# A router with its weights held still in two column halves, a re-ordered head loop, and row sums taken from the writing operations

## What is computed

```python
def layernorm(x, g, b):                    # mean and variance over the 1024 columns
    return (_normalize(x) * g + b).astype(x.dtype)

def modulate(x, shift, scale):
    return (_normalize(x) * (1.0 + scale) + shift).astype(x.dtype)
...
    merged = jnp.concatenate([rmsnorm(lru_out, norm_lru_g), rmsnorm(attn_out, norm_attn_g)], axis=-1)
    return merged @ w_out
...
    # router, for each of 256 tokens: 4 groups and 32 experts, 36 logits
    g_prob = jax.nn.softmax((xc @ w_rg + b_rg), axis=-1)
    g_top, g_idx = lax.top_k(g_prob, 1)
    e_logits = (xc @ w_re + b_re).reshape(-1, N_GROUPS, EXPERTS_PER_GROUP)
    e_in = jnp.take_along_axis(e_logits, g_idx[:, :, None], axis=1)[:, 0]
    e_top, e_loc = lax.top_k(jax.nn.softmax(e_in, axis=-1), EXPERT_TOPK)
    # two experts a token, each a gated hidden layer of 256, weighted and summed
...
        x = layernorm(DEEPNORM_ALPHA * x + g1 * mix, ln1_g[l], ln1_b[l])
        u2 = modulate(x, sh2, sc2)
        ffn = hierarchical_moe(u2, ...)
        x = layernorm(DEEPNORM_ALPHA * x + g2 * ffn, ln2_g[l], ln2_b[l])
```

## Time and profile before

| | us |
|---|---|
| median of 3 runs (lowest, highest) | 1044.45 (1040.17, 1044.59) |
| the profiled execution | 1041.96 |
| its span in the trace | 1039.5 |
| TensorE busy | 998.6 |
| VectorE busy | 586.4 |
| ScalarE busy | 351.8 |

### The profile page before, as it was taken

The page is one execution under the profiler, slowest core; times in us unless marked ns, Lnnn a source line. Parts: engine busy times, 40 slices in busy tenths (PEclk is TensorE's granted clock), DMA queues, the critical chain, the costliest instruction groups (busy, mean ns, idle before and its releaser), DMA issues.

```text
span 1039.5 us, 15072 instructions
## 1 busy us (share of the span) xinstructions
PE 998.6 (96%) x5378; PEld 608.9 (59%) x5378; DVE 586.4 (56%) x1104; ACT 351.8 (34%) x676; POOL 20.3 (2%) x41
## 2 busy tenths in 40 slices
PE   8999999999999999999999999989999999999985
PEld 7678556978878534434434579867763343433434
DVE  5834436555345546454454575886765755555556
ACT  5654325346334222222222365743521111111113
POOL 1000001000000000000000000000000000000000
PEclk9999999999998999999999999998899999999998
DMA  9263591456408399999999729530709999999931
GB/s 364 113 258 126 211 416 63 162 191 235 162 24 368 152 378 426 427 424 426 424 427 424 314 82 364 203 122 1 283 10 367 427 425 424 426 424 427 425 157 42
DMA packets 28896, 289.06 MB, mean 278 GB/s; under 512 B 3080, under 2 KB 5544, under 8 KB 7728
## 3 DMA queue, kind: packets, MB, share of 16 engines
q1 hardware_dynamic: 25344, 282.04, 65.9%
q0 software_dynamic: 1136, 3.74, 1.1%
q10 hardware_dynamic: 2368, 2.64, 0.8%
HBM read 287.34 MB, written 1.06 MB: 277 GB/s over the span
## 4 chain that ended last, share of the span: by engine, by line
PE 55%; DVE 7%; ACT 2%; issue 1%; DVEq 0%; ACTq 0%
PE bank L981 22%; PE bank L995 11%; PE bank L1001 6%; PE bank L988 4%; PE bank L626 2%; PE bank L628 1%; PE bank L627 1%; DVE ring_r L483 1%; PE bank L603 1%; PE bank L1103 1%; PE bank L954 1%; PE bank L1104 1%; PE bank L1056 1%; PE bank L925 1%; PE bank L1092 0%
## 5 line engine op out<-in xcount | busy, mean ns | idle before, releaser
L981 PE MATMUL bank<-ring,arena 128*64 128x512 f32 x1040 | 237.5, 598 | 1.4 <-DVE arena L2224 1.4
L2238 DVE TENSOR_REDUCE arena<-bank 128x512 f32 x130 | 83.8, 686 | 117.2 <-PE bank L1001 114.7
L483 DVE TENSOR_TENSOR ring_r<-ring,ring_r 128x1024 fp32r<-128x1024 f32 (+1 forms) x84 | 99.2, 1212 | 84.7 <-ACT ring_r L476 84.7
L981 PEld LDWEIGHTS bank<-ring,arena 128*64 128x64 f32 x1040 | 69.3, 136 | 123.8 <-issue 123.8
L995 PE MATMUL bank<-ring,arena 128*64 128x512 f32 x520 | 125.8, 604 | 0.5 <-DVE arena L2253 0.3
L476 ACT ACTIVATE ring_r<-ring 128x1024 fp32r<-128x1024 f32 (+1 forms) x84 | 85.0, 1046 | 76.9 <-PE bank L628 75.1
L626 PE MATMUL bank<-HT_r,ring_r 128*128 128x256 f32 x352 | 101.6, 289 | 3.5 <-DVE ring_r L483 1.8
L628 PE MATMUL bank<-HT_r,ring_r 128*128 128x256 f32 x352 | 99.6, 283 | 0.0
L1574 ACT ACTIVATE arena<-bank 128x512 f32<-128x512 f32 x64 | 38.3, 598 | 150.8 <-PE bank L981 150.8
L1001 PEld LDWEIGHTS bank<-tab,arena 128*128 128x128 f32 x520 | 55.7, 140 | 54.8 <-issue 49.6
L1001 PE MATMUL bank<-tab,arena 128*128 128x128 f32 x520 | 70.9, 279 | 3.3 <-DVE arena L2267 2.1
(11 more groups left out here) (431 smaller groups left out, 1427.9 us busy)
## 6 DMA issues: line engine op xcount, KB each, us to landing
ring<-in_experts SPq DMA_DIRECT2D x64, 2048.0 KB, 15.1
ring<-in_experts SPq DMA_DIRECT2D x64, 1024.0 KB, 11.5
ring<-in_ada SPq DMA_DIRECT2D x12, 2048.0 KB, 10.4
ring<-in_win SPq DMA_DIRECT2D x5, 2048.0 KB, 13.0
ring<-in_hy SPq DMA_DIRECT2D x3, 2048.0 KB, 19.7
ring<-in_mk SPq DMA_DIRECT2D x2, 2048.0 KB, 13.2
ring<-in_mv SPq DMA_DIRECT2D x2, 2048.0 KB, 10.5
ring<-in_wo SPq DMA_DIRECT2D x2, 2048.0 KB, 7.5
```

Of the source, the lines that this page charges most:

```text
L483: nc.vector.tensor_tensor(R(w), w, R(h), ALU.subtract).then_inc(sem("w_low"), 1)
L981: last = mm(gu_bank[g:g + WIN, :], xw[:, k, :], w[:, k * 512:(k + 1) * 512], start=k < 2, stop=k >= KD - 2)
L2238: last = V.reduce_sum(ysT[:, 4 * u:4 * u + 4, bass.ds(s, WIN)], dT_bank[u][:, :].rearrange("p (c g w) -> p c w g", c=4, g=2), AXX)
```

## The change

Five things are edited. The router product takes eight products of 256 tokens, with 64 columns of weights held still (36 of this k, the rest of the next, whose results are not read), even and odd k in the two column halves. ScalarE copies the result to `turned`, and two products with the table `stack` add the two halves and turn tokens back to the partitions, in a stage of its own (`rl`, bank 3). xn_high, xn_low and the weights w1, w2 move in the orders of ScalarE and VectorE. The number of `occupy` products changes in four places. The orders of ScalarE and VectorE in the head loop are others. The row sums of two norms come from the operations that write X.

```diff
 def moe(b):   # TensorE
-                    occupy("rT2", 0, 19)
+                    occupy("rT2", 0, 17)
...
                 for k in range(KD):
                     ready(pe, f"rT{b}", k // 2)
-                    for t in range(TT):
-                        last = mm(ps[:, t * 64:t * 64 + G + NE], HT[:, k, t * P:(t + 1) * P], w[:, k, :],
-                                  start=k + t == 0, stop=k == KD - 1 and t == TT - 1)
+                    g = 64 * (k % 2)
+                    n = min(64, KD * (G + NE) - k * (G + NE))
+                    last = mm(ps[g:g + n, 0:S], wr[:, b - 1, k * (G + NE):k * (G + NE) + n], HT[:, k, :],
+                              start=k < 2, stop=k >= KD - 2)
                 full(last, f"rt{b}")
+                ps = take(pe, f"rl{b}")
+                ready(pe, f"rt{b}")
+                for t in range(TT):
+                    last = mm(ps[:, t * 64:t * 64 + G + NE], turned[:, t * P:(t + 1) * P], stack[:, 0:G + NE],
+                              start=True, stop=True)
+                full(last, f"rl{b}")
                 if b == 1:
                     ada_col(9)
-                occupy(f"cnt{b}", 0, 10 if b == 2 else 6)
+                occupy(f"cnt{b}", 0, 10 if b == 2 else 8)
@@ TensorE, beside(h)
-                elif h == 3:
-                    occupy("ap2", 0, 4)
                 elif h in (4, 5):
                     if h == 4:
-                        occupy("ap2", 0, 4)
+                        occupy("ap2", 0, 2)
@@ ScalarE, moe(b)
-                for t in range(TT):
-                    A_(R(xn_high[:, t, :]), XN[:, t, :], ACT.Copy).then_inc(sem("xn_high"), 1)
+                A_(R(xn_high[:, 0, :]), XN[:, 0, :], ACT.Copy).then_inc(sem("xn_high"), 1)
+                ps = got(act, f"rt{b}")
+                free(A_(turned, ps[:, 0:S], ACT.Copy), f"rt{b}")
+                A_(R(xn_high[:, 1, :]), XN[:, 1, :], ACT.Copy).then_inc(sem("xn_high"), 1)
@@ ScalarE, head loop
+                if h in (2, 4, 6):
+                    attention_out(h // 2 - 1)
+                if h == 5:
+                    high(act, "wp1", (2,))
                 if h + 2 < H1:
                     a_exp(h + 2)
-                if h in (2, 4, 6):
-                    attention_out(h // 2 - 1)
...
-                if h == 5:
-                    high(act, "wp1", (2,))
@@ ScalarE, statistics(i, t): the next two go, and all four (i, t) are done here
-                link(A_(junk2, X[:, t, :], ACT.Copy, accum_out=sum_z[i, t]))
-                A_(mean_z[i, t], sum_z[i, t], ACT.Copy, scale=-1.0 / D).then_inc(sem("mean"), 1)
@@ VectorE, moe(b): split_low(t) is L2118 and L2119 for one t
+                split_low(0)
+                ps = got(dve, f"rl{b}")
...              (the chain to M12, m2 and cand4)
+                split_low(1)
...
-                (the wait for the exponentials and L2154 to L2159)
                 ps = got(dve, f"cnt{b}")
...              (counts, places, sel)
+                (the wait for the exponentials and L2154 to L2159, now ahead of selw)
@@ VectorE, wp_attention(t)
                     free(V.scalar_tensor_tensor(out=x, in0=ps[:, :], scalar=rstd_a[:, t:t + 1], in1=x,
-                                                op0=ALU.mult, op1=ALU.add), *MIX[t, u])
+                                                op0=ALU.mult, op1=ALU.add, accum_out=(sum_z, half_z)[u][1, t]), *MIX[t, u])
                 for u in range(2):
                     ready(dve, *MIX[t, u])
+                V.tensor_scalar(mean_z[1, t], sum_z[1, t], half_z[1, t], -1.0 / D, ALU.add, ALU.mult).then_inc(sem("mean"), 1)
@@ VectorE, head loop, behind probT2 and a_norm(h + 1)
+                if h == 3:
+                    dve.wait_ge(sem("roots"), upto(ROOTS, "lru"))
+                    wp_lru(0, (0,))
+                    wp_lru(0, (1,))
                 if h + 2 < H1:
                     a_max(h + 2)
                 h = 0: gate_weights(0, 2)                      (as before)
-                h = 1: gate_weights(0, 3), low(wp1, 0 and 1), gate_weights(1, 2), gate_weights(1, 3), lss
+                h = 1: low(wp1, 0), gate_weights(0, 3)
-                h = 2: attention_low(0), low(wp0, 2), wp_lru(0, 0)
+                h = 2: lss, gate_weights(1, 2), attention_low(0)
-                h = 3: wp_lru(0, 1), low(wp0, 3)
-                h = 4: attention_low(1)
+                h = 4: low(wp1, 1), attention_low(1), low(wp0, 2), gate_weights(1, 3)
-                h = 5: low(wp1, 2)
+                h = 5: low(wp0, 3), low(wp1, 2)
                 h = 6: attention_low(2), low(wp1, 3), wp_lru(1, 0)   (as before)
                 h = 7: wp_lru(1, 1), asa                             (as before)
@@ VectorE, mid_norm(t) and behind it
                 V.scalar_tensor_tensor(out=X[:, t, :], in0=XN[:, t, :], scalar=rstd_n[1][:, t:t + 1],
-                                       in1=ROW[:, 1024:2048], op0=ALU.mult, op1=ALU.add).then_inc(sem("x_mid"), 1)
+                                       in1=ROW[:, 1024:2048], op0=ALU.mult, op1=ALU.add, accum_out=sum_z[2, t]
+                                       ).then_inc(sem("x_mid"), 1)
                 dve.wait_ge(sem("x_mid"), t + 1)
+                V.tensor_scalar(mean_z[2, t], sum_z[2, t], -1.0 / D, None, ALU.mult).then_inc(sem("mean"), 1)
-            moments_of(2, 1)
```

More of the change, by code:

```diff
@@ L193, in _moe_stages @@
     one = b == 1
-    return [(f"rT{b}", 4)] + [("adac8", 1)] * one + [(f"rt{b}", 1)] + [("adac9", 1)] * one \
+    return [(f"rT{b}", 4)] + [("adac8", 1)] * one + [(f"rt{b}", 1), (f"rl{b}", 1, (3,))] + [("adac9", 1)] * one \
         + [(f"cnt{b}", 1)] + [("bias", 1)] * one + [(f"gx{b}", 8), (f"swT{b}", 2)] \
@@ L370, in two_blocks @@
         oneh, relb, brow = HTf[:, 0:512], HTf[:, 512:512 + H1], HTf[:, 1024:1536]
+        turned = area(0, S)
         route_at = at + 6656
@@ L918, in moe @@
                 pe.wait_ge(sem("wr"), 16 * b)
-                w = three(wr[:, b - 1, :], KD)
                 ps = take(pe, f"rt{b}")
@@ L1742, in statistics @@
                 A_(dev_n[i][:, t:t + 1], ssq_z[i, t], ACT.Sqrt, scale=1.0 / D, bias=eps_2).then_inc(sem("dev"), 1)
-            for t in range(TT):
-                for u in range(2):
-                    ready(act, *MIX[t, u])
-                statistics(1, t)
-            act.wait_ge(sem("x_mid"), 1)
-            statistics(2, 0)
-            deviation_of(2, 1)
+            for i in (1, 2):
+                for t in range(TT):
+                    statistics(i, t)
             link(A_(idle, eps_2, ACT.Exp))
@@ L2116, in moe, with split_low @@
                 channel_evac(f"rT{b}", HT, 4, gain, shift)
-                for t in range(TT):
+                def split_low(t):
                     dve.wait_ge(sem("xn_high"), TT * (b - 1) + t + 1)
@@ L2124, in moe @@
                 lg = three(ps[:, 0:128], TT)[:, :, 0:G + NE]
-                free(V.tensor_tensor(L, lg, biasr[b - 1].unsqueeze(1).broadcast_to([P, TT, G + NE]), ALU.add), f"rt{b}")
-                ready(dve, f"rt{b}")
+                free(V.tensor_tensor(L, lg, biasr[b - 1].unsqueeze(1).broadcast_to([P, TT, G + NE]), ALU.add), f"rl{b}")
+                ready(dve, f"rl{b}")
                 lgg = L[:, :, 0:G]
@@ L2175, in moe @@
                                            op0=ALU.is_equal, op1=ALU.add).then_inc(sem(f"sel{b}"), 1)
+                dve.wait_ge(sem("e_exp"), b)
+                dve.wait_ge(sem("g_exp"), b)
+                link(V.reduce_sum(gsum, gex, AXX))
+                link(V.reciprocal(pgrp, gsum))
+                link(V.tensor_scalar(w2, ex2, 1.0, None, ALU.add))
+                link(V.reciprocal(w1, w2))
+                link(V.tensor_tensor(w1, w1, pgrp, ALU.mult))
+                link(V.tensor_tensor(w2, w1, ex2, ALU.mult))
                 for t in range(TT):
@@ L2568, in _ @@
                     gate_weights(0, 2)
-                if h == 1:
+                elif h == 1:
+                    low(dve, "wp1", (0,))
                     gate_weights(0, 3)
-                    low(dve, "wp1", (0, 1))
-                    gate_weights(1, 2)
-                    gate_weights(1, 3)
-                if h == 2:
-                    low(dve, "wp0", (2,))
-                if h == 1:
+                elif h == 2:
                     ps = got(dve, "lss")
                     free(V.tensor_copy(ssq_a[:, 2:4], ps[:, 0:2]), "lss")
-                if h in (2, 3):
-                    dve.wait_ge(sem("roots"), upto(ROOTS, "lru"))
-                    wp_lru(0, (h - 2,))
-                if h == 3:
+                    gate_weights(1, 2)
+                    attention_low(0)
+                elif h == 4:
+                    low(dve, "wp1", (1,))
+                    attention_low(1)
+                    low(dve, "wp0", (2,))
+                    gate_weights(1, 3)
+                elif h == 5:
                     low(dve, "wp0", (3,))
-                if h == 5:
                     low(dve, "wp1", (2,))
-                if h == 6:
```

(15 more changed lines are left out.)

17 lines of the change are left out of this document (3 added, 14 removed).

## The result

| | us |
|---|---|
| kernel before, median of 20 runs (lowest, highest) | 1040.37 (1038.09, 1044.59) |
| changed kernel, median of 20 runs (lowest, highest) | 1036.9 (1035.65, 1040.05) |
| ratio, with its 95% interval | 0.9971 (0.9961 to 0.9982) |
| profiled execution of the changed kernel, its span | 1036.54, 1034.5 |

The change makes the kernel 0.3% faster; 1.4% was forecast (14.85 us). About 3.5 us of the gain are there. The three runs that the prediction started from also lay high: with more runs the kernel before has 1040.37, not 1044.45. So it is luck that 1036.9 still lies at the edge of the forecast's 1025 to 1037.5, a span that was counted from 1044.45. By the forecast's own classes a change of 0.3% is none that can be told (within 0.5%), which had a chance of 0.07.

A forecast was written before the change was run, and what follows sets the result against it. TensorE was taken to set the expert loops' pace, and waits to bound the stretches ahead. Gains summed to 14.85 us off the profiled 1041.96, 1027.1; with the median 2.5 us higher, 1029.6, range 1025 to 1037.5 (8 in 10).

The forecast's parts named there:

- head loop: Head loop: VectorE's new order starts `wp_lru(1, 0)` 8.05 us sooner; with full clock and two short waits, 8.3 us gained.
- norms: Norms ahead of the second routing: row sums from writing operations cost 0.15 us, between 0.45 gained and 0.7 lost.
- second routing, logits and counts: Second routing: new router product brings logits 2.15 us sooner; counts, with filler ending before `hot`, gain 0.8 us.
- first routing, logits and counts: First routing: logits come 2.05 us sooner; counts, no longer behind slow-clock filler, gain 1.7 us.
- the term of 3.75: First routing: the gain of its logits and counts together, 3.75 us.
- two of 0.25 and 0.4 us: Head loop: short new waits, 0.25 us for `low(wp1, 1)` in h = 4, 0.4 us for head 5's copy.
- Rival (b): Routings: TensorE's clock falls there anyway, so fillers run slow; 2 us lost in each, 1033.6 us; 22%.
- Rival (c): Head loop: VectorE's heap moves from h = 1 to h = 4 to 6; gain only 4.8 us, 1033.1; 13%.
- late copies: Heads 4 to 6: copies L2558 late by over 1 us in the changed profile would mean rival (c).
- Rival (d): Expert loops: loads set their ends, so an earlier start only waits; no change beyond 0.5%, 1040 to 1044; 7%.
- Rival (e): Head loop: with fewer fillers the clock falls in head 3 and stays at half; slower, 1045 to 1058 us; 4%.
- The norms' unknown: Norms: cost of six accumulator sums on the path, bounded by nothing and 0.19 us each, taken as 0.1 each.

The follow-up runs named there:

- e4: Changed kernel with the first routing's bias product and its ScalarE copy moved behind the gathering products; 1032.74 us, ratio 0.9931 to the kernel before.
- e10: Changed kernel with the first routing's bias product and its copy moved behind the turned weights; 1033.81 us, ratio 0.9925 to the kernel before.
- e11: e10 with ten filler products instead of six ahead of the first routing's gathering; 1030.55 us, ratio 0.9906 to the kernel before.
- e5: The changed kernel itself, unchanged, run and profiled again; 1037.42 us, ratio 0.9979 to the kernel before.
- e7: Changed kernel with the third product group of head 6 moved whole to head 7; 1035.97 us, ratio 0.9965 to the kernel before.
- e12: e11 with head 6's third product group moved to head 7, no fillers in heads 0 and 1; 1030.46 us, ratio 0.9903 to the kernel before.
- e2: Kernel before with only the head loop's new ScalarE and VectorE orders and changed fillers; 1036.18 us, ratio 0.9967.
- e3: The norms' run: kernel before with only the norms' row sums from the writing operations, statistics on ScalarE and rT2's filler; 1041.22 us, ratio 1.0009.
- e1: Kernel before with only the router part (router product, turning, moved xn_high, xn_low, w1, w2, cnt1's filler); 1039.39 us, ratio 0.9986.

## Why the prediction was wrong

The direction came as forecast, and the size did not. Two steps failed, both mainly by what stands beside the change and not in it. "Profiled execution" compares one execution of each kernel; the medians differ by 3.5 us only.

| term | forecast | profiled execution |
|---|---|---|
| head loop | 8.3 | 2.3 |
| norms | -0.15 | 0.56 |
| second routing, logits and counts | 2.15 + 0.8 | 2.18 + 1.03 |
| first routing, logits and counts | 2.05 + 1.7 | 0.2 of 4.0 |
| clock falls at 110 to 170 us | none | -1.0 |
| sum | 14.85 | 5.3 (span: 5.0) |

**First failed step: the first routing.** "A DMA of a table (onehot) is issued when the router product is full and so moves along; only a product that nobody on this path awaits needs it." The issue did move along, but that nobody awaits a product's result says nothing of who is queued behind it: in TensorE's order filler and gathering stood behind it, and neither began before it. The timeline of the kernel before had the row that shows how near this was:

```profile
331.02 0.52 POOL L2726 DMA_DIRECT2D HT<-in_rel_bias  x1
...
338.29 1.02 PE L943 MATMUL bank<-HT 33*8 33x512 f32 x2
```

The load took 7.2 us from its issue, so it landed at 338.2, just as TensorE came to the product; it had no wait to show. With the old routing a wait of 0.59 us did show in the norms' run, where the clock fell only behind the router product (3.73 us instead of 5.18) and TensorE came sooner:

```profile
337.69 1.02 PE L943 MATMUL bank<-HT 33*8 33x512 f32 x2 [0.59 <-DMA HT<-in_rel_bias]
```

Now the load is issued 3.2 us sooner (328.81 against 331.02 + 1.01), takes 9.1 at a DMA share of 1.00, and lands 1.3 us sooner, while TensorE comes 4 us sooner. The 5.47 us of slow filler, which I took as gained, had been its cover. Experiments e4, e10 and e11 show it. From the router product's start to loop 1 are 30.68 us before and 30.47 and 31.51 in the changed kernel; with nothing but this product out of the way 29.97, with product and copy off the path 28.51, with the clock kept up too 26.89. So the term of 3.75 was right for a routing without this product (3.8), and with it 0.2 and -0.8 were measured.

**Second failed step: the head loop's 8.3 us.** They were summed from rows of one execution in which heads 0 and 1 ran at full clock. At full clock the sum was nearly right: 51.13 - 44.27 = 6.9, and the bank wait in head 6 makes 1.3 more, 8.2 in all. In the profiled execution 4.67 of the 8.3 went in the slow stretch (10.62 less 5.95) and 1.40 in the bank wait, which leaves the 2.3 that were measured. Where the clock falls in heads 0 and 1, which it did in 5 of the 8 profiled executions of the new order without filler there (the changed kernel, e5, e7, e10, e12; not e2, e4, e11), the old order hides that fall under VectorE's lateness at head 3, loses 0.2 to 0.7 us there and even keeps its clock in head 3 (e3 and e1); the new order pays it in full. Then new against old is 47.4 to 49.0 against 48.9 to 49.4. The prediction had a rival with a clock fall, but in head 3 and in the routings, places where the trace of before showed one, and none in heads 0 and 1.

The missed wait in head 6: I looked for waits on VectorE's copies and on `low`, and found two of 0.25 and 0.4 us; I did not ask who reads the banks out in head 6. VectorE came to `attention_low(2)` at 718.39, behind the two `low` of h = 5 and the copy of head 6, while TensorE was done with its work ahead of the bank at 717.52.

**What held.** The router product takes 1.95 us at both places (forecast 1.8), and the turning with its copy 0.38 + 0.61. The Trainium skill ("TensorEngine Tiling (Array Packing)", section "Tiling Modes") has an array that drains at a change of mode. With the changes in and out here the product took 0.15 us more than by the rate taken from the earlier trace rows, and the logits came within 0.03 us of the forecast's gain, so no larger cost of a drain can be seen. w1 and w2 behind `sel` cost nothing: from the reading of the counts to the second loop are 17.02 us (before 16.97). The second routing's 3.2 us came as summed, but in part by luck: sum and check went by the same execution, whose old product ran in a clock fall. The prediction laid its 0.165 us a record to the weights loaded; at full clock it was 0.117 (3.73 for 32), and against such executions 1.2 to 1.6 us are gained. Rival (b), the clock falling in the routings, was right for the first (0.50 at 336 to 342) and wrong for the second (1.00 at 738 to 758). Rival (c) came in part: in heads 4 to 6 VectorE's moved work makes TensorE wait for a bank, 1.40 us of the 3.5 that the rival had. The sign that it named, late copies, is there too (head 5's starts at 712.76, 3.5 us behind its turn), but TensorE waits for none of them. Rival (d) did not come: the second loop follows its routing at once and at its old pace. Rival (e) had a fall in the head loop, but in head 3, for another reason, and of another size.

The norms' unknown was the accumulator. The Trainium skill ("VectorE: DVE Perf Modes", section "Two Vector instructions with no wait between them") has two instructions for it, and the trace agrees: there is a DVE_READ_ACCUMULATOR for each. It takes 0.08 us and mostly lies over its operation's end (730.18 against 729.50 + 0.75), so six cost nearly nothing, and the whole stretch came out 0.7 us shorter than summed.

**Still open.** Why the clock falls in heads 0 and 1 in some executions and not in others isn't settled. Kernels with the same head loop show both, but no kernel's traces do: of the changed kernel there are two, both with the fall. E10's six runs, of which one has a trace, differ as if of both kinds. What share of all executions has the fall, and so how the medians come about, isn't known. The medians of e4 and e11 lie 4.7 and 6.9 us under e5's, and the first routing gives 1.5 and 4.6 of that; rarer falls in the heads would fit the rest, but no run shows it. The old order with no fall at all was not seen, so what the re-ordering is worth with the clock kept everywhere is not measured. Issuing the table's load earlier, the other way to mend the first routing, wasn't tried.

## What to carry to other kernels

When a step comes earlier, list everything that stands between it and its user in the queue of the same engine, also what nobody on the path waits for, and ask what each of these waits for and whether that moves as far. Compare from a mark in the same kernel (here the router product's start), not from the start of the span, and read a term from more than one execution where the clock fell in it. Slack ahead of a wait may be cover for something: before a wait is taken out, ask what the stretch ahead of it costs in a bad execution, and compare new with old under the same clock. Work without a use in a thin stretch pays where it fills a wait (ten fillers ahead of the first gathering), and costs as much as it brings where the engine has work anyway (heads 0 and 1).

## What the runs showed of the hardware

- VectorE's accumulator was read in 0.08 us, under half of ScalarE's 0.19.
- A load of 1 KB issued from GpSimd's queue 0.55 us behind one of 256 KB, while the experts' loads held the DMA share at 1.00, landed 9.1 us after its issue in the changed kernel and 7.2 before; the one of 256 KB took 8.0 and 6.5.
- The old router product, 32 records of 128x36 with 128x128 of weights each, took 3.73 us at full clock (e2, second routing) and 5.28 with a fall in it (before); the new one, 16 records of 128x256 in column halves, 1.95.
- At the half clock two records of 33x512 took 1.87 us, at the full one 1.02; 32 gathering records took 7.56 us at full clock, and 9.15 with a fall in them.
- In e10's six runs the mean granted clock parts the times: 1028.11 to 1030.49 us at 0.996 to 0.997, 1033.3 to 1035.05 at 0.989 to 0.990. In the changed kernel's 20 runs it does not: 1036.0 and 1039.01 us both at 0.990, 1035.65 to 1039.37 at 0.987.
